# A two-layer hybrid network on one core: the last top-k rounds of the selected attention move from units 0 to 11 into units 0 to 2

## The reference

```python
def dsa_attention(q, k, v, q_idx, k_idx, w_idx, top_k, scale):   # top_k = 128
    rel = relu(einsum('bqhd,bkd->bqhk', qi_blk, k_idx))
    score = einsum('bqhk,bqh->bqk', rel, w_blk)
    score = where(key_pos <= qpos, score, -inf)
    _, idx = top_k(score, top_k)            # each query keeps 128 keys
    ...                                     # softmax attention over these keys
for l in range(2):
    h = rms_norm(x, norm1[l]); proj = h @ w_in[l]
    # o_a: low-rank causal, o_b: sliding window, o_c: dsa, o_d: causal with forget gates
    x = x + concatenate([o_a, o_b, o_c, o_d]) @ w_out[l]
    x = x + square(relu(rms_norm(x, norm2[l]) @ w_up[l])) @ w_down[l]
```

## Time and profile before

| | |
|---|---|
| median of three runs | 4183.71 us (4181.35 to 4184.64) |
| the profiled execution, its own time | 4184.64 us |
| its span in the profile | 4183.0 us |
| TensorE busy | 3902.5 us, 93% |
| VectorE busy | 1559.6 us, 37% |
| ScalarE busy | 853.3 us, 20% |
| attention stage of the first layer | about 2805 to 2922 us |
| attention stage of the second layer | about 3595 to 3712 us |

### The profile page before, as it was taken

The page is one execution under the profiler, slowest core; times in us unless marked ns, Lnnn a source line. Parts: engine busy times, 40 slices in busy tenths (PEclk is TensorE's granted clock), DMA queues, the critical chain, the costliest instruction groups (busy, mean ns, idle before and its releaser), DMA issues.

```text
span 4183.0 us, 93995 instructions
## 1 busy us (share of the span) xinstructions
PE 3902.5 (93%) x40200; PEld 2505.8 (60%) x40200; DVE 1559.6 (37%) x3295; ACT 853.3 (20%) x1872; POOL 774.1 (19%) x634
## 2 busy tenths in 40 slices
PE   5999999989988888888999999999999999999998
PEld 4544444455567777777444434447688854658887
DVE  1411111154544445544222212444344424525363
ACT  2200000020044555554200001115000011430000
POOL 3100000000033334333000000000334410013343
PEclk9999999999999999999999999999999999999999
DMA  8389999942200000000379997110122221102221
GB/s 346 117 319 351 360 357 356 373 184 74 84 7 12 13 12 13 16 13 12 141 312 428 429 428 297 61 61 1 61 101 81 81 89 41 41 21 81 96 86 41
DMA packets 56386, 627.08 MB, mean 150 GB/s; under 512 B 5905, under 2 KB 9233, under 8 KB 20497
## 3 DMA queue, kind: packets, MB, share of 16 engines
q1 hardware_dynamic: 49664, 599.41, 36.1%
q0 software_dynamic: 3968, 14.16, 1.2%
q10 hardware_dynamic: 2448, 9.05, 0.6%
HBM read 604.50 MB, written 18.09 MB: 149 GB/s over the span
## 4 chain that ended last, share of the span: by engine, by line
PE 84%; issue 5%; DVE 5%; DMA 4%; ACT 1%; DVEq 1%; PEld 0%; SPq 0%; POOL 0%; ACTq 0%; PEldq 0%; POOLq 0%
PE bank L914 64%; PE bank L1415 14%; DMA ring<-slabs 2%; DMA work<-slabs 2%; PE bank L1799 1%; PE bank L942 1%; PE bank L1807 1%; PE bank L1816 1%; PE bank L1466 1%; DVE work L2849 0%; DVE hx L2526 0%; PE bank L1805 0%; PE bank L1802 0%; DVE resc L2747 0%; PE bank L1260 0%
## 5 line engine op out<-in xcount | busy, mean ns | idle before, releaser
L914 PE MATMUL bank<-ring,work 128*32 128x256 f32 (+3 forms) x7002 | 764.3, 438 | 66.9 <-DMA ring<-slabs 58.6
L914 PE MATMUL bank<-work 128*128 128x256 f32 (+7 forms) x3478 | 713.1, 416 | 13.1 <-DVE work L3213 4.8
L914 PEld LDWEIGHTS bank<-work 128*128 128x128 f32 (+3 forms) x3478 | 463.4, 178 | 246.8 <-issue 185.5
L914 PEld LDWEIGHTS bank<-ring,work 128*32 128x32 f32 (+2 forms) x7002 | 316.6, 123 | 489.4 <-issue 388.8
L914 PE MATMUL bank<-hx,ring 128*128 128x512 f32 (+1 forms) x1344 | 484.3, 514 | 4.8 <-DVE hx L2526 2.8
L914 PE MATMUL bank<-work,ring 128*128 128x256 f32 (+1 forms) x1616 | 479.3, 455 | 7.1 <-DVE work L2791 3.4
L914 PEld LDWEIGHTS bank<-work,ring 128*128 128x128 f32 x1616 | 306.2, 190 | 174.4 <-issue 133.5
L1415 PE MATMUL bank<-work 64*64 64x64 f32 x11520 | 327.9, 227 | 71.1 <-issue 60.2
L914 PEld LDWEIGHTS bank<-hx,ring 128*128 128x128 f32 x1344 | 253.5, 190 | 223.5 <-issue 201.5
L3411 POOL TENSOR_TENSOR work<-ring 128x512 f32<-128x512 f32 (+1 forms) x44 | 69.4, 1578 | 1620.5 <-ACT work L2028 1223.0
L1415 PEld LDWEIGHTS bank<-work 64*64 64x64 f32 x11520 | 294.7, 139 | 97.8 <-issue 95.3
(11 more groups left out here) (335 smaller groups left out, 4845.6 us busy)
## 6 DMA issues: line engine op xcount, KB each, us to landing
ring<-slabs SPq DMA_DIRECT2D x228, 2048.0 KB, 9.9
work<-slabs SPq DMA_DIRECT2D x48, 2048.0 KB, 18.3
work<-kv SPq DMA_DIRECT2D x18, 384.0 KB, 3.1
kv<-work SPq DMA_DIRECT2D x2, 3072.0 KB, 15.7
kv<-work ACTq DMA_DIRECT2D x6, 512.0 KB, 17.1
work<-tabs ACTq DMA_DIRECT2D x1, 2176.0 KB, 8.9
resx<-xT SPq DMA_DIRECT2D x1, 2048.0 KB, 10.9
kv<-work POOLq DMA_DIRECT2D x1, 2048.0 KB, 7.1
```

The lines of the kernel that those rows point to most:

```text
L914: return pe.matmul(out, lhsT, rhs, start=(k == 0), stop=(k == n - 1))
```

## The change

In units 0 to 11 one round for `ranks[3]` stood behind the second minimum. Now two rounds stand behind the second and two behind the fourth minimum of units 0, 1 and 2; the count stays twelve. The step "keep 3" moves from behind unit 12 to behind unit 3, in the written order and in the code.

```diff
@@ -221,7 +221,7 @@
-    AT_DVE += [("red", _u + 1, _h) for _h in range(HEADS)] * _more + [("ev", _u)] + [("keep", 3)] * (_u == 12)
+    AT_DVE += [("red", _u + 1, _h) for _h in range(HEADS)] * _more + [("ev", _u)] + [("keep", 3)] * (_u == 3)
@@ -3179,10 +3179,10 @@
                     for h in range(HEADS):
                         if u + 1 < len(ATTENTION):
                             lowest(u + 1, h)
-                        if u < 12 and h == 1:
-                            rounds(3, 1)
+                        if u < 3 and h % 2:
+                            rounds(3, 2)
                     rows_out(u)
-                    if u == 12:
+                    if u == 3:
                         hidden(3)
```

## The result

The changed kernel takes 4206.05 us (median of five runs, 4203.79 to 4214.46); the kernel before, with two more runs on the same chip counted in, 4183.71 (median of five runs, 4170.25 to 4187.63). The ratio is 1.0062, with a 95% interval of 1.0042 to 1.0082: slower, by 26 us taken as a ratio and 22 as a difference of the medians. The forecast was 20.4 us slower.

A forecast was written before the change was run, and what follows sets the result against it. TensorE was taken to bound the attention stage; per layer 7.5 us of queue plus 1.1 and 1.6 us of clock falls, doubled to 20.4 us, on 4183.71 gave 4204.1 us, range 4196.0 to 4209.0.

The forecast's parts named there:

- That TensorE bounds the stage: First layer's attention, 2804 to 2922 us: TensorE's waits are only 1.3, 0.7, 0.5 and 0.3 us; second layer the same.
- The queue on VectorE and the three stalls: Units 0 to 2: added rounds delay scaled rows, so TensorE stalls 3.59 us, then 1.65 and 2.28 us more.
- So the pure queue costs 7.5 us per layer: Attention, units 0 to 2: total delay from VectorE's queue without any clock effect, 7.5 us per layer.
- the price of a round: VectorE: 1.60 us from one round to the next, 1.58 up to a following minimum; two rounds 3.18 us.
- VectorE has no spare time there even now: Unit 0, kernel before: second pair of minima at 2811.56 starts right behind the round begun at 2809.98.
- After the third it is the whole 1.6 us: Behind unit 2's stall: a fall of TensorE's clock costs 1.6 us per layer.
- After the first stall ... 1.1 us: Behind unit 0's stall: a clock fall costs 1.1 us per layer, 0.48 us of it being hidden.
- The rounds fit into VectorE's idle time: Rival, 2804 to 2838 us: 16.7 us idle hold nine rounds' 14.3 us, no change, 4183.7 us; chance 0.06.
- No fall of the clock: Rival, behind the stalls: TensorE stays at 2.4 GHz, 15.0 us slower, 4198.7 us; none or one fall, chance 0.24.
- Three falls: Rival, units 0 to 2: clock falls behind all three stalls, 23.6 us slower, 4207.3 us; chance 0.19 (or somewhat more).
- Faster: Rival, sliding-window units: exponentials come sooner without rounds between minima, at most 2.3 us gained; chance 0.01.
- The Trainium skill's rule: TensorE's gaps between matmul bursts: idle lowers the clock; taken for each of three gaps, it gives three falls.

The follow-up runs named there:

- g_filled_less: Changed kernel with 3, 1 and 2 unread matmuls on TensorE ahead of its wait for the scaled rows of units 0, 1 and 2; ratio 1.0044.
- the repeat: The changed kernel run once more without any edit; ratio 1.0050.
- f_keep_late: Changed kernel with the keep step back behind unit 12; ratio 1.0065.
- j_first_filled: Changed kernel with three unread matmuls on TensorE in the first stall only, the third left empty; ratio 1.0062.
- k: Kernel before, with four rounds in unit 2 and one each in units 0, 1 and 3 to 8, keep behind unit 12; ratio 1.0027.

## Why the prediction was right or wrong

**That TensorE bounds the stage, and that the twelve rounds were free before: right.** Without them the stage was 0.04 to 0.07 us shorter.

**The queue on VectorE and the three stalls: right in place and mechanism, a little too long.** "So the pure queue costs 7.5 us per layer": measured 6.6 to 6.8, in g_filled_less. Worked out were 3.59 us for the first stall, measured 3.03. The step that was off is the price of a round: "1.58 us up to a minimum that follows (2809.98 to 2811.56)". In that row the minimum started when its logits had come, not when the round was over. TensorE's timeline of before shows it:

```profile
2808.61 0.71 PE L1807 MATMUL bank<-work,tabs_sb 128*128 128x128 f32 x4
...
2811.04 0.71 PE L1807 MATMUL bank<-work,tabs_sb 128*128 128x128 f32 x4
```

The minima at 2809.14, which waited for logits by their bracket, start 0.53 us behind the first of these rows; those at 2811.56 start 0.52 us behind the second. A row without a bracket can thus have waited too, here for about 0.14 us, and the prediction's "VectorE has no spare time there even now" was wrong by as much. The true distance is 1.44 us, and two rounds are 3.04. What follows the scaled rows also starts 0.34 instead of 0.44 us after them.

**"After the third it is the whole 1.6 us": this is the term that failed.** In the result the clock's falls were placed rightly, behind the first and the third stall and not behind the second. But their price was taken from rows where the clock came back soon. In the trace of before, between 30 and 4170 us, the record of the clock has 29 stretches at the low level, 26 of 3.4 us and three of 6.8. Behind the third stall it was low for 13.7 us in the result's first layer. Against g_filled_less, the way from L1834 of unit 2 to the end of the stage took 6.0 us more there (96.60 against 90.64 us), where 1.6 had been put; in the second layer, with 3.4 us of low clock, it took 1.7 us more, as forecast. "After the first stall ... 1.1 us" was too small as well: L1834 of unit 2 came 1.6 us later than in g_filled_less in the first layer (low for 3.4 us) and 2.5 us later in the second (low for 6.8). In all the clock cost 7.5 and 4.1 us in the result's two layers and 3.3 and 7.4 in the repeat's; I had 2.7 per layer, and 4.3 as the bound above.

So the forecast was 20.4 us made of 15.0 and 5.4; measured are 25.0 in the stages, made of 13.4 and 11.6. The two errors partly cancel, which is luck. On the ratio, 1.0062 of 4183.71 is 4209.6 us, just above the range's 4209.0; the median of 4206.05 us lies in it.

**The rivals.** "The rounds fit into VectorE's idle time": refuted. Over the stretch they do fit by the sum, yet the scaled rows come late in each unit. "No fall of the clock": refuted by the stretches at 0.50, and g_filled_less measures that case: 13.4 us against the rival's 15.0. "Three falls" comes closest in time, 23.6 us, and for a wrong reason: there were two in each layer, one of the four long. "Faster": nothing came back from units 3 to 11. Nor did the second layer's fall at the end of attention vanish in the result.

**The Trainium skill's rule** on idle gaps (page "TensorE: Matmul & The Clock Gate", section "Why this matters for your kernels") held as a warning. Its row is on gaps above a least length, which the prediction left out when it took the rule for each of the three gaps; here the clock fell behind 1.98 us and not behind 0.88. As a measure of the loss the length of the gap misleads: 3.02 us was followed by 0 to 6.8 us at the low clock, 1.98 us by 3.4 to 17.1 where unit 3's small matmuls followed.

**The keep step** at nothing: right, f_keep_late.

The runs point to no placing that beats the kernel before: with all twelve rounds for nothing the stage would be 0.07 us shorter at most.

## What to carry to other kernels

Work that is hidden on a half-idle engine is paid for by the slack of each single hand-over, not by the sum of idle time: here six added rounds, one in each of six units, cost 2.8 us in a layer without a fall of the clock, and nine, three in each of three units, cost 6.6, though by the sum the idle time would have held them.

When such a stall falls on TensorE, look at the granted clock behind it and at what TensorE does there: 2 us of stall ahead of many small matmuls cost up to 7 us more through the clock (j_first_filled, second layer: 97.89 us from L1834 of unit 2 to the end of the stage, 90.66 in g_filled_less). If a stall can't be avoided, a few unread matmuls in it, sized to be done before it ends, keep the clock up (stage 123.0 instead of 126 to 130), but they are dear if they outlast it (127.5).

Before a distance between two rows is taken as a price, check on the other engine, and not in the bracket alone, that the second wasn't waiting for something else.

## What the runs showed of the hardware that was not expected

- The granted clock stayed at its low level for 10.2 to 17.1 us in ten layers, with TensorE busy for 10.00 of 10.00 and 11.00 of 11.00 us (k and j), in matmuls of 64 to 256 columns.
- The same stall, to 0.05 us, had between 0 and 6.8 us (first, 3.01 to 3.06 us) or, with unit 3's matmuls behind it, 3.4 and 17.1 us (third, 1.98 us) of low clock behind it, in two layers of one execution as well as between executions.
- A MAX8 and MATCH_REPLACE8 round over 512 columns takes 1.60 us up to the next round and 1.44 us up to another kind of instruction without a drain.
